# Last two experts of each stage: the order of combine, gather and down products

## The reference

```python
def expert_block(args):
    toks, e = args
    xb = x[toks]
    hb = jax.nn.silu(xb @ w1[e]) * (xb @ w3[e])
    return hb @ w2[e]

y = lax.map(expert_block, (row_tok.reshape(n_blk, MOE_BLOCK), blk_exp))
y = y.reshape(R, D).astype(jnp.float32) * row_w[:, None]
out = jnp.zeros((M, D), jnp.float32).at[row_tok].add(y)
```

## Time and profile before

| | us |
|---|---|
| median of 3 runs | 1629.74 (1626.6 to 1630.58) |
| profiled execution | 1628.12 |
| its span, first to last instruction | 1626.4 |
| TensorE busy (matmuls) | 1356.7, 83% |
| VectorE busy | 696.9, 43% |
| ScalarE busy | 244.5, 15% |
| mean granted TensorE clock | 0.919 of 2.4 GHz |
| bytes moved | 528.53 MB, 325 GB/s over the span |

### The profile page before, as it was taken

One profiled execution on the slowest core, in us unless ns is written; L12 is line 12 of the kernel. 1 busy time (PEld: TensorE's weight loads), 2 busy tenths in 40 slices (PEclk: granted clock), 3 DMA queues, 4 the chain that ended last, 5 costly groups with the idle time before them and its releaser, 6 DMA issues. The chain is left out here.

```text
span 1626.4 us, 27590 instructions
## 1 busy us (share of the span) xinstructions
PE 1356.7 (83%) x11866; PEld 890.9 (55%) x11866; DVE 696.9 (43%) x1848; ACT 244.5 (15%) x501; POOL 75.6 (5%) x116
## 2 busy tenths in 40 slices
PE   7999789898789789679999999999796666566666
PEld 6645456565456556368766847887353333333333
DVE  4634556222233324226587734662363333233224
ACT  2321330110011112032211212211200000000000
POOL 2400100000000000030000100010000000000000
PEclk9999899999899889889999999999898788788877
DMA  9952799999999999985633343564999999999996
GB/s 337 267 207 104 293 359 421 414 421 417 417 411 415 421 414 417 397 286 212 254 117 116 99 153 141 203 211 172 408 393 428 428 428 430 428 427 428 430 423 251
DMA packets 104376, 528.53 MB, mean 325 GB/s; under 512 B 10344, under 2 KB 29048, under 8 KB 78144
## 3 DMA queue, kind: packets, MB, share of 16 engines
q1 hardware_dynamic: 99360, 522.50, 80.0%
q0 software_dynamic: 2400, 4.13, 1.3%
q10 hardware_dynamic: 2496, 0.15, 0.1%
HBM read 525.69 MB, written 1.06 MB: 324 GB/s over the span
## 5 line engine op out<-in xcount | busy, mean ns | idle before, releaser
L1430 PE MATMUL ps<-weight_ring,e_xT 128*32 128x256 f32 x3456 | 259.3, 465 | 159.1 <-DMA weight_ring<-in_w_up_dram 91.4
L1430 PEld LDWEIGHTS ps<-weight_ring,e_xT 128*32 128x32 f32 x3456 | 139.2, 133 | 275.4 <-issue 229.9
L1715 DVE TENSOR_TENSOR e_g<-e_act_g,ps 128x128 f32<-128x128 f32 x64 | 24.9, 389 | 267.6 <-ACT e_act_g L1519 266.4
L1519 ACT ACTIVATE e_act_g<-ps 128x128 f32<-128x128 f32 x64 | 17.7, 277 | 614.1 <-PE ps L1430 614.1
L1713 DVE TENSOR_TENSOR e_act_g<-e_act_g,ps 128x128 f32<-128x128 f32 x32 | 9.2, 287 | 228.8 <-ACT e_act_g L1519 228.8
L1457 PE MATMUL ps<-weight_ring,e_gT 128*32 128x256 f32 x1568 | 94.8, 382 | 5.4 <-DVE e_gT L1719 2.0
L1430 PE MATMUL ps<-expert_set,e_xT 128*32 128x256 f32 x640 | 52.0, 496 | 43.8 <-DMA expert_set<-in_w_up_dram 43.8
L2237 PE MATMUL ps<-expert_set,weight_ring 128*128 128x256 f32 x384 | 84.2, 379 | 0.0
L2237 PEld LDWEIGHTS ps<-expert_set,weight_ring 128*128 128x128 f32 x384 | 73.0, 190 | 9.9
L1398 PE MATMUL ps<-e_y,e_GwT 32*128 32x256 f32 x1024 | 74.5, 405 | 1.8 <-DVE e_y L1747 1.2
L1390 PE MATMUL ps<-e_n,e_Gt 128*32 128x256 f32 x1056 | 72.5, 392 | 0.9 <-DVE e_Gt L1638 0.7
(11 more groups left out here) (572 smaller groups left out, 1883.8 us busy)
## 6 DMA issues: line engine op xcount, KB each, us to landing
weight_ring<-in_expert_w_dram SPq DMA_DIRECT2D x89, 2048.0 KB, 20.4
weight_ring<-in_w_in_dram SPq DMA_DIRECT2D x26, 2048.0 KB, 9.0
weight_ring<-in_w_gate_dram SPq DMA_DIRECT2D x19, 2048.0 KB, 32.8
weight_ring<-in_w_up_dram SPq DMA_DIRECT2D x19, 2048.0 KB, 37.4
weight_ring<-in_w_down_dram SPq DMA_DIRECT2D x18, 2048.0 KB, 38.6
weight_ring<-in_w_ada_dram SPq DMA_DIRECT2D x12, 2048.0 KB, 12.8
expert_set<-in_w_gate_dram SPq DMA_DIRECT2D x10, 2048.0 KB, 33.6
expert_set<-in_w_up_dram SPq DMA_DIRECT2D x10, 2048.0 KB, 38.2
```

The lines of the kernel that those rows point to most:

```text
L1430: mm = pe.matmul(ps[32 * j:32 * j + 32, 4, 0:256].rearrange("p (w f) -> p w f", w=2), xT[:, k, :], w13[:, :, k, j * P:(j + 1) * P], start= ...
L1519: act.activation(act_g[:], ps[:, 4, 0:P], gated).then_inc(s_silu, 1)
L1715: dve.tensor_tensor(g[:], spread(act_g[:]), spread(ps[:, 4, P:2 * P]), ALU.mult).then_inc(s_g, 1)
```

## The change

For experts in the run-time loop (`not known`) three things are put in another order; experts 0 to 29 keep theirs.

1. TensorE: the combine of the expert before stands between the two halves of the up products.
2. TensorE: the gather of the expert after stands behind the down products. It waits for y of this expert (count i+2 where it was i+1), and the down products no longer wait for `xg` of the next.
3. VectorE: the three instructions for `GwT` (now the helper `weights`) stand right behind `gT`, in stage 2 followed by y; `take_x` of the next expert and the bookkeeping come last.

```diff
@@ TensorE, expert(i, q, u), inside the loop over k of the up products
+                    if not known and k == KD // 2 - 1:
+                        pe.wait_ge(s_Gw, i + 1)
+                        pe.wait_ge(s_y, i + 1)
+                        combine()
                 mm.then_inc(s_up, 1)
...
-                pe.wait_ge(s_Gt, i + 2)
-                pe.wait_ge(s_y, i + 1)
-                gather()
-                if not first:
+                if known:
+                    pe.wait_ge(s_Gt, i + 2)
+                    pe.wait_ge(s_y, i + 1)
+                    gather()
+                if known and not first:
                     pe.wait_ge(s_Gw, i + 1)
                     combine()
...
                 pe.wait_ge(s_gT, i + 1)
-                pe.wait_ge(s_xg, i + 2)
+                if known:
+                    pe.wait_ge(s_xg, i + 2)
...
                 mm.then_inc(s_down, 1)
+                if not known:
+                    pe.wait_ge(s_Gt, i + 2)
+                    pe.wait_ge(s_y, i + 2)
+                    gather()
@@ VectorE, expert(i)
+                def weights(j):
+                    dve.wait_ge(s_comb, i + 1)
+                    step(j, dve.scalar_tensor_tensor(GwT[:], srow[:, 0, :], sp_[:, 0:1], wrow[:, 0, :], ALU.is_equal, ALU.mult))
+                    step(j + 1, dve.scalar_tensor_tensor(Gw2[:], srow[:, 1, :], sp_[:, 0:1], wrow[:, 1, :], ALU.is_equal, ALU.mult))
+                    dve.tensor_tensor(GwT[:], GwT[:], Gw2[:], ALU.add).then_inc(s_Gw, 1)
...
                 dve.transpose(gT[:], g[:]).then_inc(s_gT, 1)
+                if not known:
+                    weights(VO - 4)
+                    if mod is not None:
+                        dve.wait_ge(s_down, i + 1)
+                        dve.tensor_tensor(y[:], ps[:, 5, 0:256], gate_m[:], ALU.mult).then_inc(s_y, 1)
                 take_x(i + 1)
...
-                step(VO - 4, ins)
+                step(VO - 4 if known else VO - 2, ins)
...
-                dve.wait_ge(s_comb, i + 1)
-                step(VO - 3, dve.scalar_tensor_tensor(GwT[:], srow[:, 0, :], sp_[:, 0:1], wrow[:, 0, :], ALU.is_equal, ALU.mult))
-                step(VO - 2, dve.scalar_tensor_tensor(Gw2[:], srow[:, 1, :], sp_[:, 0:1], wrow[:, 1, :], ALU.is_equal, ALU.mult))
-                dve.tensor_tensor(GwT[:], GwT[:], Gw2[:], ALU.add).then_inc(s_Gw, 1)
+                if known:
+                    weights(VO - 3)
...
-                if mod is not None:
+                if mod is not None and known:
                     dve.wait_ge(s_down, i + 1)
                     dve.tensor_tensor(y[:], ps[:, 5, 0:256], gate_m[:], ALU.mult).then_inc(s_y, 1)
```

More of the change, by code:

```diff
@@ L1706, in expert @@
             def expert(i):
+                known = isinstance(i, int)
                 def step(j, ins):
```

## The result

The changed kernel takes 1633.44 us (median of 15 runs, 1630.67 to 1636.25), the kernel before 1627.0 (15 runs, 1624.52 to 1633.92). The ratio is 1.0032, 95% interval 1.0022 to 1.0043: slower by 5.2 us, between 3.6 and 7.0. That is just beyond the 0.3% that I took for the bound of what can be told.

What follows compares the result with a forecast made beforehand. Expert weight transfers bound the stages' ends, TensorE mixer 2; behind the last landing 1.8 - 0.1 + 0.6 + 1.65 = +4.0 us gives 1632.1 or 1633.7, predicted 1633.5, range 1629 to 1638.5.

Steps and rivals of the forecast that it cites:

- Landings stay, mixer 2 carries the delay: Expert 31's down weights still land at 693.5 and 1610.9; stage 1's delay passes one for one through mixer 2.
- Combine between the halves, stage 2: Expert 30 in stage 2: combine delays second half and gT by 1.2 us, down products start 0.3 us late.
- Gather behind the down products: Expert 31's gather waits for y; stage 2 first half 1601.5 to 1601.7 against 1601.23; cost 0 in both stages.
- The gain in front in stage 2: Expert 31's down products in stage 2 start at 1611.05, 1.8 us earlier; VectorE's queue eats it, leaving -0.1 us.
- The tail at full clock: After expert 31, gather and VectorE bookkeeping precede the tail: +1.8 us in stage 1, -0.1 in stage 2, before loop exits.
- Leaving the loop: VectorE's register work and branch at loop end come onto the path twice: 0.3 us each, together +0.6, between 0 and 2.7.
- The clock: TensorE idles before expert 31's down products, so its clock falls to half in one of the two stages: +1.65 us.
- Rivals 1 and 2: Expert 31's down products: clock falls in both stages, +6.5, 1636.2, chance 0.24; or holds in both, +2.3, 1632.0, chance 0.27.
- My signs of being wrong: Stage 1's tail starts before 699, mixer 2's end doesn't move with it, or expert 30/31 weights issue differently relative to expert 29.

Runs made afterwards that it cites:

- the 20 products: Changed kernel plus 20 products (40 records) between expert 31's up and down products; against the kernel before 1.0031, and again 1.005.
- the combine alone: Kernel before with only the combine moved between the halves for experts 30 and 31: 0.9987; in stage 2 alone 0.9992, there with 12 filling products 0.9995.

## Why the prediction was right, and where it was lucky

- **Landings stay, mixer 2 carries the delay.** Right. In stage 2 the last weights are issued 1.99 us behind the start of expert 29's down products, before and after. From the tail of stage 1 to the last issue in stage 2 it is 892.1 to 894.1 us in all twelve traces without the 20 products, whatever the order.
- **Combine between the halves, stage 2.** Predicted: expert 30's down products 0.3 us late. Measured from the issue: 5.93 us against 5.58, +0.35, and the row names gT.
- **Gather behind the down products.** Predicted: expert 31's first half 0.3 to 0.5 us late in stage 2, at no cost. Measured from the issue: 11.04 against 10.62 us, and the second half 15.62 against 15.57.
- **The gain in front in stage 2.** Predicted: the down products 1.8 us earlier. Measured 1.83, against the one trace that I had. There expert 31's second half ran at half clock, and I took that for the old order. At full clock the old order starts them 20.64 us behind the issue, and the gain is gone. So my price for stage 2, -0.1 us and the loop exit, fits one kind of execution only; against the other the new order's tail is 2.67 us longer.
- **The tail at full clock.** Predicted from the down products, loop exit included: 5.83 us in stage 1 and 6.33 in stage 2. Measured 6.08 and 6.51. Against the trace of before, with its late start in stage 2, that is +2.36 and +0.35 where I had +2.1 and +0.2.
- **Leaving the loop.** I took 0.3 us each between 0 and 1.36; the rows show 0.38 and 0.31 from the last slot update to the tail. The estimate of 0.2 from the page of the Trainium skill that I cited (Advanced Engine Details and Errata, Control Flow Timing) was for both exits; they take 0.7 with the register work.
- **The clock.** Size right, reason wrong. I took one fall of 1.65 us in the two stages. Over three traces of the changed kernel, down products and gather of expert 31 together, it is 2.6, 1.3 and 1.3 us, 1.7 in the mean, in 4 of 6 tails. But I had tied it to the length of the idle time, by two rows near 3.1 us and one of 2.20. The runs show half clock behind 1.88 us and full clock behind 2.96. Rivals 1 and 2 had it in both stages or in none; the three traces show both once and one of the two twice. What it costs in the time of a run stays unmeasured, since filling the gap had an effect elsewhere.
- **My signs of being wrong.** One came true by the letter: the tail of stage 1 starts at 698.55 and not behind 699. It doesn't count against the mechanism, since all of stage 1 stood over 2 us earlier in this execution; counted from the down products the tail is 7.38 us, where the bound of 699 meant 5.5. The other two didn't come true.
- **The number.** 1633.5 predicted, 1633.44 measured, but by luck in part: the three runs shown had a median of 1629.74, fifteen have 1627.0. My difference was +4.0, the measured one is +5.2 (3.6 to 7.0); by the medians alone +6.4. The traces give an estimate of both kinds of execution, with the mean of the clock, 1.7: 2.36 + 0.35 + 1.7 = +4.4 us where the old order's second half in stage 2 was at half clock, 2.36 + 2.67 + 1.7 = +6.7 where it wasn't. The measured value lies between. I gave 0.72 to within 0.3% and 0.25 to slower; the ratio, 1.0032, is just over the line.

## What to carry to other kernels

Before an instruction is moved behind the last thing that a phase waits for, ask what in the loop's last turn works for a turn that never comes: here a gather and eight VectorE instructions (nine in stage 2) that had cost nothing under the wait for the down weights and beside the down products. The tail stood behind them in VectorE's program and began 1.35 us earlier without them, though nothing waited for what they wrote. Where the path is bound by a landing, work taken out from in front of it buys nothing and leaves TensorE idle; here half clock followed in 4 of 6 cases. And before a gain is taken from one trace of the old kernel, look whether its late start is the order or that execution's clock.

## What the runs showed of the hardware

- TensorE's clock behind a wait for weights differs from one execution to the next: with 2.84 to 2.96 us of idle time in front, the six down groups of expert 31 in three traces of one kernel took 2.58, 2.60, 2.45, 1.93, 1.93 and 2.97 us. Behind 1.88 us of idle time one group took 3.62 us, behind 1.86 us another 1.93. With the combine alone, the three unfilled groups of expert 31 behind 2.06 to 2.09 us took 2.62, 2.77 and 2.80 us.
- The same holds further ahead: expert 31's second half in stage 2, in the old order, took 3.64 us behind 1.88 us of idle time in one trace and 1.93 us behind 1.43 us in the other, which moved the start of the down products by 1.6 us.
- Extra products in the gap went with full clock behind them: the five groups took 1.93 or 1.94 us.
- 40 more records on TensorE in stage 1 went with a mixer 2 that took 439.2 and 436.9 us in two traces, against 432.6 to 434.2 in twelve others, though its code is the same and the clock in expert 31's down products was full. Its cause is open.
